# Transposes by DMA for a block's second norm and its heads, with later MLP weight loads

## The reference

```python
xn = rmsnorm(x, norm_mix_g)
u = xn @ w_in                                  # (4, 4096, 5120)
# b_g, c_g, v_a: 512 columns each; q, k, v: 4 heads; g_a, g_b: gates of 1024 each
y_a = (b_g * causal_conv3(c_g * v_a)) @ w_a_out
o = softmax(q1 k1) v - lam * softmax(q2 k2) v   # two maps of d=64 per head, ALiBi, causal, v of 128
o = rmsnorm(o, subln_g) * (1 - lam_init)        # over the 128 values of a head
y_b = o @ w_b_out
x = x + (sigmoid(g_a) * y_a + sigmoid(g_b) * y_b) @ w_o
h = rmsnorm(x, norm_mlp_g) @ w_mlp_in
x = x + square(relu(h)) @ w_mlp_out             # d_ff = 4096
out = rmsnorm(x, norm_final_g)
```

## Time and profile before

| | |
|---|---|
| median of 3 runs | 1213.76 us (1213.59 to 1214.24) |
| the profiled execution | 1213.64 us |
| its span on the slowest core | 1212.1 us (cores 1207.8 to 1212.1) |
| TensorE busy | 1167.8 us (96%) |
| ACT busy | 653.0 us (54%) |
| DVE busy | 601.0 us (50%) |
| POOL busy | 81.7 us (7%) |
| granted TensorE clock | 0.995 to 0.997 of full speed |

### The profile page before, as it was taken

The page is one execution under the profiler, slowest core; times in us unless marked ns, Lnnn a source line. Parts: engine busy times, 40 slices in busy tenths (PEclk is TensorE's granted clock), DMA queues, the critical chain, the costliest instruction groups (busy, mean ns, idle before and its releaser), DMA issues.

```text
span 1212.1 us, 27519 instructions; the slowest of 8 cores (1207.8 to 1212.1 us)
## 1 busy us (share of the span) xinstructions
PE 1167.8 (96%) x7464; PEld 578.9 (48%) x7464; DVE 601.0 (50%) x971; ACT 653.0 (54%) x1055; POOL 81.7 (7%) x141
## 2 busy tenths in 40 slices
PE   4999999999999999999999999999999999999995
PEld 2455444555555555544444444444444444444443
DVE  3666336544534333333365347336455463727767
ACT  4555268889899998976746764320211112030065
POOL 1000012111111000010000000000000000000012
PEclk9999999999999999999999999999999999999998
DMA  9667220002000000059432318011230403040124
GB/s 228 197 140 178 36 36 2 3 2 38 2 3 2 2 3 2 3 88 192 105 105 44 97 16 141 3 34 30 41 63 8 71 1 70 1 70 14 23 87 191
DMA packets 16759, 71.87 MB, mean 59 GB/s; under 512 B 1984, under 2 KB 2240, under 8 KB 14176
## 3 DMA queue, kind: packets, MB, share of 16 engines
q0 software_dynamic: 6768, 35.65, 17.7%
q1 hardware_dynamic: 9696, 33.94, 8.1%
q10 hardware_dynamic: 144, 0.52, 0.1%
HBM read 97.37 MB, written 8.39 MB: 87 GB/s over the span
## 4 chain that ended last, share of the span: by engine, by line
PE 89%; DMA 3%; ACT 2%; DVE 2%; issue 2%; DVEq 0%; POOL 0%; ACTq 0%; POOLq 0%
PE ps_all L289 68%; PE ps_all L286 12%; PE ps_all L291 7%; DMA big<-w_g 2%; PE ps_all L310 2%; ACT big L588 1%; DMA big<-w_in 1%; ACT big L297 0%; DVE big L313 0%; DVE big L1108 0%; DVE big L1126 0%; PE ps_all L663 0%; DVE big L305 0%; DVE big L980 0%; DVE big L1096 0%
## 5 line engine op out<-in xcount | busy, mean ns | idle before, releaser
L289 PE MATMUL ps_all<-big 128*128 128x512 bf16 (+2 forms) x4192 | 917.6, 375 | 14.7 <-DMA big<-w_in 7.6
L289 PEld LDWEIGHTS ps_all<-big 128*128 128x128 bf16 x4192 | 394.6, 98 | 482.9 <-issue 42.5
L588 ACT ACTIVATE big<-ps_all,big 128x1024 bf16<-128x1024 f32 (+3 forms) x428 | 324.8, 802 | 37.8 <-PE ps_all L286 14.0
L1081 ACT ACTIVATE big<-ps_all 128x512 bf16<-128x512 f32 x124 | 74.0, 597 | 334.1 <-PE ps_all L289 333.9
L1108 DVE TENSOR_TENSOR big<-ps_all,big 128x512 f32<-128x512 f32 x256 | 176.6, 691 | 39.5 <-PE ps_all L289 36.1
L286 PE MATMUL ps_all<-big 128*128 128x129 bf16 x2176 | 163.6, 221 | 3.5 <-DVE big L631 1.2
L286 PEld LDWEIGHTS ps_all<-big 128*128 128x128 bf16 x2176 | 126.8, 98 | 54.1 <-issue 45.3
L1082 DVE TENSOR_TENSOR big<-big 128x512 bf16<-128x512 bf16 x124 | 52.7, 425 | 162.2 <-ACT big L1081 162.2
L291 PE MATMUL ps_all<-big 64*128 64x512 bf16 (+3 forms) x640 | 108.7, 352 | 3.6 <-ACT big L588 2.3
L297 ACT ACTIVATE big<-big 128x1024 bf16<-128x1024 f32 (+1 forms) x65 | 68.7, 1057 | 55.1 <-PE ps_all L289 25.1
L313 DVE TENSOR_TENSOR big<-ps_all,big 128x1024 bf16<-128x1024 bf16 (+1 forms) x49 | 59.0, 1205 | 45.1 <-PE ps_all L310 45.1
(11 more groups left out here) (62 smaller groups left out, 417.1 us busy)
## 6 DMA issues: line engine op xcount, KB each, us to landing
big<-xs SPq DMA_DIRECT2D x48, 512.0 KB, 7.3
big<-w POOLq DMA_DIRECT2D x16, 1024.0 KB, 13.1
big<-w_g POOLq DMA_DIRECT2D x16, 512.0 KB, 7.9
out<-big SPq DMA_DIRECT2D x15, 512.0 KB, 2.7
big<-w_in POOLq DMA_DIRECT2D x12, 512.0 KB, 8.5
big<-w_o POOLq DMA_DIRECT2D x1, 2048.0 KB, 24.2
big<-w_a POOLq DMA_DIRECT2D x1, 1024.0 KB, 10.1
big<-w_b POOLq DMA_DIRECT2D x1, 1024.0 KB, 11.1
```

What stands on the lines that cost most here:

```text
L289: S.op("pe", lambda e: e.matmul(out, lhsT, rhs, start=start, stop=stop), reads=reads, writes=writes)
L588: S.op("act", lambda e, a=a, b=b, bi=bi: e.activation(PT[:, :, a:b], Sps[:, buf, :, a:b], AF.Exp, bias=btab[:, bi:bi + 1], scale=0.125), r ...
L1081: S.op("act", lambda e: e.activation(r, ph, AF.Relu), reads=[phk], writes=[rk])
```

## The change

- The second norm's tiles and the 16 heads are turned by transposing DMAs on SP's queue (`turn_rows`). The TensorE transposes, the flips and what the planner did for them are gone; the first norm keeps `flip_rows`.
- A head is scaled by four DVE instructions of 128 columns that also multiply by the head's gain, now a row in SBUF (`gsr`): loaded by SP at the start of the attention stage and multiplied by a constant on POOL.
- The second norm's gain is multiplied in place in SBUF, four steps behind the statistics (`mul2`); the transposing DMA is issued right behind the scaling. The statistics write their squares into PSUM banks 6 and 7, no longer into the scaled rows' buffer.
- The first MLP load is emitted after step 23, `W2_0` after the third step of the MLP, `W1_1` after the seventh, the final gain after the eleventh; each of these three waits for the square of its step.
- The second merge buffer no longer waits for the heads' output buffers.

```diff
     def row_stats(x, xkey, ntok, xb, xbkey):
+        xb = xb[:ntok]
...
+    def turn_rows(xb, xbkey, dst, dkeys):
+        S.dma("sp", lambda e: e.dma_start_transpose(dst, xb), reads=[xbkey], writes=dkeys)
...
+    gsr = ar.take([128, 128], F32)
...
     wload(Wa, w_a, "Wa")
+    ld("sp", gsr, gsub_d.partition_broadcast(128), "gsr")
+    S.op("pool", lambda e: e.tensor_scalar(gsr, gsr, (1.0 - LAM_INIT) * math.sqrt(128.0), None, ALU.mult),
+         reads=["gsr"], writes=["gsr"])
...
         def fin_():
-            flip_at[n] = LAT + dve(lambda e: e.tensor_tensor(
-                on, o, ss[:, 4:8].unsqueeze(2).to_broadcast([128, 4, 128]), ALU.mult),
-                ["ato", "atrs"], [onk], 0.69, clk["pool"] + LAT)
+            for q in range(4):
+                dve(lambda e, q=q: e.scalar_tensor_tensor(on[:, q, :], o[:, q, :], ss[:, 4 + q:5 + q], gsr,
+                                                          ALU.mult, ALU.mult),
+                    ["ato", "atrs", "gsr"], [onk], 0.22, clk["pool"] + LAT)
+            i, h = steps[n]["i"], steps[n]["h"]
+            turn_rows(on.rearrange("p q v -> p (q v)"), onk,
+                      O_n[:, h, i * 512:(i + 1) * 512].rearrange("p (q t) -> p q t", q=4), ["qo%d_%d" % (i, h)])
         yield (fin_, "pool")
-
-    def emit_flip(n):
...
-        if flips and side["whole"] and flip_at.get(flips[0], BIG) <= t and b7["free"] <= t:
-            set_mode(0)
-            emit_flip(flips.pop(0))
-            continue
-        if flips and flip_at.get(flips[0], BIG) <= t and side["whole"]:
-            r_side = BIG
...
-    S.reuse(["mT1_%d" % d for d in range(8)], at_keys)
+    S.reuse(["mT1_%d" % d for d in range(8)], [k_ for k_ in at_keys if k_ not in ("aton0", "aton1", "gsr")])
...
-    pst_ring = Ring([bank_bf_T(6), bank_bf_T(7)], "pst", keys=["pb6", "pb7"])
+    junk = bank(6, 2)
+    S.reuse(["pb6"], ["pb7"])
...
-            rest_flips()
...
-            st2[T] = (xb, xbkey) + row_stats(x, "xm%d" % T, 128, xb, xbkey)
+            st2[T] = (xb, xbkey) + row_stats(x, "xm%d" % T, 128, junk, "pb6")
...
-        else:
+        elif name == "post2":
             xb, xbkey, st, skey = st2[T]
-            flip_rows(xb, xbkey, 128, gmlp, "cst", xn2T_all[:, :, T * 128:(T + 1) * 128],
-                      ["xn2T_%d" % T, "ya%d" % i] + ["qo%d_%d" % (i, h) for h in range(4)], pst_ring)
+            xT = xn2T_all[:, :, T * 128:(T + 1) * 128]
+            turn_rows(xb, xbkey, xT, ["xn2T_%d" % T, "ya%d" % i] + ["qo%d_%d" % (i, h) for h in range(4)])
+        if name == "mul2":
+            xT = xn2T_all[:, :, T * 128:(T + 1) * 128]
+            S.op("dve", lambda e: e.tensor_tensor(xT, xT, gmlp.unsqueeze(2).to_broadcast([128, 8, 128]), ALU.mult),
+                 reads=["xn2T_%d" % T, "cst"], writes=["xn2T_%d" % T])
...
-            for name, off in (("act2", 0), ("dve2", 1), ("post2", 2)):
+            for name, off in (("act2", 0), ("dve2", 1), ("post2", 1), ("mul2", 4)):
...
-        for nm in ("post2", "dve2", "act2"):
+        for nm in ("mul2", "dve2", "post2", "act2"):
...
-        if j == 27:
+        if j == 23:
...
             load_w1(0)
-            load_w2(0)
-            load_w1(1)
     S.reuse(["gfin"], ["Wo"])
-    ld("sp", gfin, gfin_d.partition_broadcast(128), "gfin")
...
             mlp_in(0, sl, fc)
+            if fc == 3 and sl in (0, 1):
+                key = "h2_0_2_%d" % sl
+                wk = ("W2_0", "W1_1")[sl]
+                S.reuse([wk], [key])
+                (load_w2, load_w1)[sl](sl)
+            if fc == 3 and sl == 2:
+                S.reuse(["gfin"], ["h2_0_2_2"])
+                ld("sp", gfin, gfin_d.partition_broadcast(128), "gfin")
```

More of the change, by code:

```diff
@@ L215, in build_program @@
     lam_d = din("lam", [1, 256])
+    gsub_d = din("gsub", [1, 128])
     gfin_d = din("gfin", [1, D_MODEL])
@@ L227, in build_program @@
     cst = pers.take([128, 48], F32)
-    gmix, gmlp, bgate, convw, gsub0 = cst[:, 0:8], cst[:, 8:16], cst[:, 16:32], cst[:, 32:44], cst[:, 44:45]
+    gmix, gmlp, bgate, convw = cst[:, 0:8], cst[:, 8:16], cst[:, 16:32], cst[:, 32:44]
     nbgate = pers.take([128, 16], F32)
-    gsub = pers.take([128, 8], F32)
     lams = pers.take([128, 8], F32)
@@ L490, in build_program @@
                  reads=["lams"], writes=["lams"])
-            S.op("dve", lambda e: e.tensor_scalar_mul(gsub[:, 1:2], gsub0, (1.0 - LAM_INIT) * math.sqrt(128.0)),
-                 reads=["cst"], writes=["gsub"])
         run_evs(j)
@@ L520, in build_program @@
     OB_KEYS = ["pb4", "pb5", "pb6"]
-    Tps = bank(7).bitcast(BF16)[:, 0:512].rearrange("p (q t) -> p q t", q=4)
     S.op("dve", lambda e: e.memset(Ops[:, 2, 2, :], 1.0), writes=["pb6"])
@@ L621, in build_program @@
     o_free = [0.0, 0.0, 0.0]
-    flip_at = {}
     def evict_o(n):
@@ L652, in fin_ @@
         def fin_():
-            flip_at[n] = LAT + dve(lambda e: e.tensor_tensor(
-                on, o, ss[:, 4:8].unsqueeze(2).to_broadcast([128, 4, 128]), ALU.mult),
-                ["ato", "atrs"], [onk], 0.69, clk["pool"] + LAT)
-        yield (fin_, "pool")
-    def emit_flip(n):
-        st = steps[n]
-        i, h = st["i"], st["h"]
-        on, onk = at["on"][st["hid"] % 2], "aton%d" % (st["hid"] % 2)
-        for qc in range(4):
-            S.op("pe", lambda e, qc=qc: e.transpose(Tps[:, qc, :], on[:, qc, :], ident),
-                 reads=[onk, "ident"], writes=["pb7"])
-        clk["pe"] += 0.35
-        b7["free"] = LAT + dve(lambda e: e.tensor_scalar_mul(
-            O_n[:, h, i * 512:(i + 1) * 512].rearrange("p (q t) -> p q t", q=4), Tps, gsub[:, 1:2]),
-            ["pb7", "gsub"], ["qo%d_%d" % (i, h)], 0.48, clk["pe"] + LAT)
+            for q in range(4):
[5 more added lines that the diff above has]
+                      O_n[:, h, i * 512:(i + 1) * 512].rearrange("p (q t) -> p q t", q=4), ["qo%d_%d" % (i, h)])
+        yield (fin_, "pool")
     b7 = dict(free=0.0)
@@ L799, in build_program @@
     chains, late = [], []
-    flips = []
     def set_mode(m):
@@ L893, in build_program @@
                 chains.append(dict(gen=chain(pv_n), next=None))
-                flips.append(pv_n)
             pv_n += 1
@@ L926, in load_x_mid @@
                   writes=["xm%d" % T])
-    def rest_flips():
-        while flips:
-            emit_flip(flips.pop(0))
-        S.reuse(xb2_ring.keys, ["aton0", "aton1"])
     def gates_step(i, k):
```

9 lines of the change are left out of this document (6 added, 3 removed).

## The result

| | before | after |
|---|---|---|
| median of 4 runs | 1213.71 us (1213.59 to 1214.24) | 1202.31 us (1201.0 to 1202.39) |
| ratio to before | | 0.9900 (95%: 0.9888 to 0.9912) |
| the profiled execution | 1213.64 us | 1202.39 us |
| its span, slowest core | 1212.1 us | 1200.8 us (cores 1196.1 to 1200.8) |

The change makes the kernel 11.4 us faster; the forecast was 11.7. First the page of after: the busy time of each engine, and two of its groups (busy us, mean ns of one, idle before it).

What follows compares the result with a forecast made beforehand. Stages were taken as paced by TensorE's work. Gains of 8.8 (second norm) and 4.0 (attention), 12.8, less 1.1 paid, net 11.7: 1213.7 - 11.7 = 1202.0 us, chance 0.66, range 1198.5 to 1212.

Steps and rivals of the forecast that it cites:

- Second norm: z tiles and MLP start: transposes off TensorE's queue give 7.2 us, vanished waits for scaled rows 1.6, sum 8.8.
- The multiply by the gain: Second norm on DVE: the gain multiply in SBUF, 1024 columns, takes 1.2 us, between 0.85 and 1.39.
- The tie at the two z banks: z tiles: DVE's chain until a bank is free, 3.46 us, ties with TensorE's 3.45; 0.5 us charged, between 0 and 2.8.
- The transfers by themselves: Second norm: a 256 KB transposing DMA lands in 4 us; the schedule bears up to 6.0, so no cost.
- Rival (c): Second norm: the transposing transfer is slow by itself, slower overall from 8.0 us per transfer, 1245 us if 13.1; chance 0.14.
- Attention: Attention stage: TensorE mostly sets the pace, so removing the heads' transposes (4.6 us) gains 4.0 us, between 0 and 6.
- Rival (a): Attention stage gives nothing, because ACT takes over the pace or the new order is no better; 1206 us, chance 0.12.
- The four scalings: Heads on DVE: four short scalings take some 0.25 us each, together 1.0, for 1.18 us of removed work; cost nothing.
- Merge buffer: Second merge buffer: its narrower release gives nothing, as first use is a whole gate step after the last head's work.
- The place of the loads: First MLP loads: spreading them costs nothing; a W2 load still under way might make the second W1 some 2 us late.
- Gain row: Start of attention: gain row load and POOL multiply make the first mask slightly late; 0.3 us, between 0 and 3.
- Gate weight wait: TensorE's 2.1 us wait for a gate weight: the transfer ends at its own time, so 0.3 us saved ahead comes back.

Runs made afterwards that it cites:

- e7: Changed kernel with the first step's exponentials of each of the 16 heads computed twice on ACT; 1218.03 us, ratio 1.0054 to the kernel before.
- e4: Changed kernel with the first query-key products of each of the 16 heads issued twice on TensorE; 1203.86 us, ratio 0.9924 to the kernel before.
- e10: Changed kernel in the same order, one DVE multiply of 512 columns per head for four short ones, head's gain left out; 1197.02 us, ratio 0.9861 to before.
- e1: Changed kernel with the second merge buffer again waiting for all attention scratch, the heads' output buffers included; 1220.43 us, ratio 1.0059 to the kernel before.
- e2: Changed kernel with the first three MLP loads and the final gain asked for together again, before the second pass's z tiles; 1216.75 us, ratio 1.0027 to before.
- e11: Changed kernel with the head's gain row loaded and multiplied early, in the projection stage, in its own place; 1200.73 us, ratio 0.9894 to the kernel before.
- e8: Kernel before, with one row tile's final-norm multiply moved from POOL to DVE; 1212.13 us, ratio 0.9987 to the kernel before.
- e3: Changed kernel with only the second norm's and the loads' parts, heads turned on TensorE and scaled as before; 1202.96 us, ratio 0.9914 to the kernel before.
- e6: Changed kernel with one scaling per head, the gain multiplied once into Wb on DVE, no gain row; 1208.17 us, ratio 0.9966 to the kernel before.
- e9: e6 with the Wb multiply one DVE instruction earlier, W1_1 and W2_0 loads re-placed, gain column in existing space; 1201.17 us, ratio 0.9901 to the kernel before.
- e12: e9 with the 2 MB Wo load asked for after the fourth gate step; 1196.69 us, ratio 0.9852 to the kernel before.

## Why the prediction was right, and where it was not

The forecast of 1202.0 us met 1202.31, by its main step and by errors that cancel. By the table of stages, the 3.7 us for attention (4.0 less 0.3) did not come, and 3.4 came that I had not counted: 1.1 before the z tiles (0.8 gained where 0.3 was charged), 0.7 in the second norm (9.0 for 8.3), 1.5 and 0.1 at the end. That these nearly cancel is luck.

- **Second norm: right.** Forecast 8.8 us, measured 6.2 + 2.8 = 9.0. The z tiles run at 3.46 against 3.45, the waits at the MLP's start are gone.
- **The multiply by the gain: right.** Taken 1.2 us, measured 1.22. The tie at the two z banks ended well: the charge of 0.5 us was 0.
- **The transfers by themselves: right, and better than taken.** 2.8 us against 4. Rival (c) would have needed more than 8. "VectorE: DVE Perf Modes" of the Trainium skill, "The three transpose paths", gives 1309 ns for one block; adding up eight would have been 10.5 us. The measurement decides: eight blocks land in 2.8 us, so the page's figure is no price per block.
- **Attention: wrong.** The step that failed reads "ACT's exponentials idled 37.8 us in this stage, [...] so mostly TensorE sets the pace". The runs show mostly the opposite: 17.3 us more of ACT make all cores 16.0 us slower on the mean (e7), and 3.5 us more of TensorE 1.4 (e4), on three cores nothing. Rival (a) was right of this kernel, but only in part of the mechanism: with one scaling for four (e10) the stage did shorten by 4 us. What can be gained there is ACT's gaps, and they hang on the chain of scaling, eviction, PSUM bank and value products. Whether those 4 us come from TensorE's flips or from the flips' evictions on DVE, which went at the same time, no run tells apart.
- **The four scalings: mis-sized.** "[A] quarter at least 0.19, with start cost some 0.25, together 1.0" measured 352 ns each and 1.73 for the four, start to next start. The count against two removed multiplies was also the wrong test: what counts is not DVE's sum but what stands right ahead of the next head's eviction, and that grew from one instruction to four. In the Trainium skill the section "The TRN2 errata — SBUF-src ops pay a fixed extra latency per instruction" of "VectorE: DVE Perf Modes" warns of many small tiles; its formula for an fp32 tensor_tensor add, (128 + 151) / 0.96 = 291 ns, would make 1.16 us for four by my estimate, and the row is higher. The page has checked it at 512 and 2048 columns of another instruction, so it may not hold here.
- **Merge buffer: wrong.** "The merge buffer's narrower release gives nothing: its first use is a whole gate step after the last head's work" took for granted that the transfer lands as if nothing ran beside it. The last head's transfer takes 25.6 to 29.3 us beside the gate weights and Wo; e1 costs 18 us. The prediction had a row for this, the row loads queued among gate weights, 22.4 us, and used it only as a bound for the second norm.
- **The place of the loads: wrong in its reason.** I asked only whether the weights would be late, and set the transposes' meeting with one load instead of three at no price. e2: 14.3 us.
- **Gain row: under-sized.** Forecast 0.3 with a range to 3; e11 gains 1.6 (0.9 on the mean of all cores), and e4's core 5 shows 2.2 us at the first mask.
- **Gate weight wait: wrong sign.** Charged 0.3 as "a transfer that ends at its own time"; it vanished. Before, five of the eight cores had it, 0.7 to 2.1 us, and the three others passed that stretch in 88.1 us; after, none has it and all take 88.5. So it was worth 0.8 us on the median core and 2.0 on the slowest. It was there in the three kernels that turn the heads on TensorE (before, e8 and 1.7 us in e3) and gone in after and the seven versions that keep its four scalings or its gain row; it came back in e6 (0.4 us, one core) and e9 (4.6 us) and was gone in e12, where the Wo load was moved away. By which road the heads' part removes it, no run isolates.

## What to carry to other kernels

An engine's idle time does not tell that another one sets the pace: double a little of its work, and of the other's, and see whose time follows. When transposes go from TensorE to DMA, look not at the transfer alone but at who loads weights then, and keep every buffer that such a transfer reads out of others' waits; a 2.4 us transfer became one of 29. And if DVE has to split an instruction to do the new layout's work, count the start cost of each piece at the place where a PSUM bank waits behind it.

## What was unexpected of the hardware

- A DMA transpose of 128 KB lands in 2.4 us as a rule in the attention stage (4.4 at most) and in 25.6 to 29.3 us among weight loads from POOL's queue; with the 2 MB load moved away (e12), in 8.9 to 11.1. A tile of 256 KB took 16.3 us beside four loads (e2), and beside one W2 load 3.1 to 11.5 by core (e6).
- The 256 KB transposes of the z tiles land in 2.7 to 2.8 us in after, whose transposed rows start at byte 2688 of a partition (42 x 64, by the kernel's allocations), and in 3.0 to 3.1 where every buffer lies 32 bytes further (e3, e6); in e9, with the 32 bytes taken back, again in 2.7, and in e11, with 512 more, too.
- A DVE multiply of 0.28 us takes 2.26 us beside a POOL multiply of 2.36 that began 0.24 us earlier, and 0.28 when it begins 0.1 us ahead of it.
- A stall of TensorE of 16 us costs about 2 us more in clock: granted 0.50 over the next 4 us, then 0.72 over 4 more (e1).
